# Splitting the first output projection by tokens, with more fill pieces around the small steps and weight splits in quarters

## What is computed

```python
h = _rmsnorm(x, p['norm_mix_pre'])
c = h @ p['w_in']                       # RWKV-7 columns | q k v of attention | two gates
y_a, s_new, shift_new = _rwkv7(c_a, shift_prev, s0, ...)     # per-token matrix state
o = _rmsnorm(softmax(q1 k1) v - lam * softmax(q2 k2) v, p['subln'])
g_a, g_b = jnp.split(jax.nn.sigmoid(g_in + p['b_gate']), 2, axis=-1)
mix = g_a * (y_a @ p['w_out_a']) + g_b * (o @ p['w_out_b'])
x = x + _rmsnorm(mix @ p['w_o'], p['norm_mix_post'])
u_g, u_v = jnp.split(_rmsnorm(x, p['norm_ffn_pre']) @ p['w_ffn_in'], 2, axis=-1)
x = x + _rmsnorm((jax.nn.silu(u_g) * u_v) @ p['w_ffn_out'], p['norm_ffn_post'])
```

## Time and profile before

| | us |
|---|---|
| three timed runs | 1061.17, 1060.76, 1056.54 (median 1060.76) |
| the profiled execution | 1061.27 |
| its span | 1059.4 |
| TensorE (PE) busy | 1008.6 (95%) |
| VectorE (DVE) busy | 488.9 |
| GpSimd (POOL) busy | 486.7 |
| ScalarE (ACT) busy | 275.9 |
| idle time of POOL ahead of w_hi splits, waiting for PE to free a slot | 427.4 |

### The profile page before, as it was taken

The page is one execution under the profiler, slowest core; times in us unless marked ns, Lnnn a source line. Parts: engine busy times, 40 slices in busy tenths (PEclk is TensorE's granted clock), DMA queues, the critical chain, the costliest instruction groups (busy, mean ns, idle before and its releaser), DMA issues.

```text
span 1059.4 us, 21826 instructions
## 1 busy us (share of the span) xinstructions
PE 1008.6 (95%) x8886; PEld 950.9 (90%) x8886; DVE 488.9 (46%) x877; ACT 275.9 (26%) x782; POOL 486.7 (46%) x327
## 2 busy tenths in 40 slices
PE   5999999999889998999999998999999999999997
PEld 4999999977768887878799998999999999999996
DVE  5566799377767455555345254233233332200003
ACT  4223444354433133332211254101001010011111
POOL 3555565432215123142146812655556555566571
PEclk9999999999989999999899999999999999999999
DMA  8222323422213110103313621323232232323332
GB/s 265 61 81 80 84 76 81 132 82 71 65 42 87 33 32 13 53 32 116 110 35 128 189 58 41 99 80 98 79 94 84 81 97 79 92 79 88 92 91 85
DMA packets 137581, 89.16 MB, mean 84 GB/s; under 512 B 5242, under 2 KB 129504, under 8 KB 137504
## 3 DMA queue, kind: packets, MB, share of 16 engines
q1 hardware_dynamic: 128980, 72.65, 24.0%
q10 hardware_dynamic: 8524, 15.42, 4.2%
HBM read 78.86 MB, written 9.19 MB: 83 GB/s over the span
## 4 chain that ended last, share of the span: by engine, by line
PE 81%; DVE 12%; ACT 3%; issue 2%; POOL 1%; DMA 1%; ACTq 0%; DVEq 0%; SPq 0%; POOLq 0%
PE dense L958 65%; PE side L1028 3%; PE side L1148 1%; PE side L910 1%; PE side L874 1%; PE side L884 1%; DVE amax L1635 1%; PE side L1071 1%; PE side L940 1%; DVE otok L1662 1%; DVE early L1650 1%; PE side L864 1%; DVE gt L1756 1%; DVE early L1651 1%; DVE AR L1823 1%
## 5 line engine op out<-in xcount | busy, mean ns | idle before, releaser
L700 POOL TENSOR_SCALAR w_hi<-w_raw 128x1024 fp32r<-128x1024 f32 x117 | 126.8, 1084 | 438.4 <-PE dense L958 427.4
L958 PE MATMUL dense<-h_hi,w_hi 128*128 128x272 f32 (+2 forms) x1392 | 305.9, 297 | 7.3 <-DVE h_lo L1570 5.8
L958 PE MATMUL dense<-h_hi,w_lo 128*128 128x272 f32 (+2 forms) x1392 | 296.5, 291 | 0.0
L958 PE MATMUL dense<-h_lo,w_hi 128*128 128x272 f32 (+2 forms) x1392 | 295.9, 290 | 0.0
L703 POOL TENSOR_TENSOR w_lo<-w_raw,w_hi 128x1024 fp32r<-128x1024 f32 x117 | 286.3, 2447 | 9.8
L958 PEld LDWEIGHTS dense<-h_hi,w_hi 128*128 128x128 f32 x1392 | 223.5, 191 | 18.2 <-issue 6.6
L958 PEld LDWEIGHTS dense<-h_lo,w_hi 128*128 128x128 f32 x1392 | 224.5, 191 | 0.0
L958 PEld LDWEIGHTS dense<-h_hi,w_lo 128*128 128x128 f32 x1392 | 223.1, 192 | 0.0
L958 PE MATMUL dense<-S,w_hi 128*128 128x272 f32 (+2 forms) x648 | 109.2, 289 | 0.0
L958 PEld LDWEIGHTS dense<-S,w_hi 128*128 128x128 f32 x648 | 92.1, 188 | 0.1
L958 PE MATMUL dense<-S,w_lo 128*128 128x272 f32 (+2 forms) x324 | 68.2, 288 | 0.0
(11 more groups left out here) (266 smaller groups left out, 1412.9 us busy)
## 6 DMA issues: line engine op xcount, KB each, us to landing
w_raw<-in_w_ffn_in SPq DMA_DIRECT2D x44, 512.0 KB, 3.7
w_raw<-in_w_in SPq DMA_DIRECT2D x43, 512.0 KB, 3.9
w_raw<-in_w_ffn_out SPq DMA_DIRECT2D x16, 448.0 KB, 3.6
gates<-gst ACTq DMA_DIRECT2D x16, 272.0 KB, 2.0
w_raw<-in_w_o SPq DMA_DIRECT2D x8, 512.0 KB, 4.3
w_raw<-in_w_ffn_out SPq DMA_DIRECT2D x8, 512.0 KB, 3.7
mb<-gates ACTq DMA_DIRECT2D x1, 2176.0 KB, 10.7
ga<-gates ACTq DMA_DIRECT2D x1, 2176.0 KB, 10.2
```

Source lines behind the costliest of these rows:

```text
L700: nc.gpsimd.tensor_scalar(hi, w_raw[:, slot, :], 1.0, 0.0, ALU.mult, ALU.add).then_inc(hi_split, 1)
L958: ins = pe.matmul(acc[:, bk, 0:tn], w, r[:, t0:t0 + tn], start=first and n == 0, stop=final and n == 2)
```

## The change

1. **Fill pieces.** gB and gA quarters are one list, and attention takes 37 of them where it took 32; `turns` gives the 12 places of the last tile 12 pieces where it gave 7. `ofin` takes four fillers where it took five. New fillers stand behind `final` of tile 3, behind `tok` of the sample tile and ahead of its `wu`.
2. **Reciprocals.** For tiles 0 to 2 `yrs` moves from behind `yvar` to the row of `ya`, one level step later; `yfin` comes one place later, behind `ya`.
3. **Output projection by tokens.** Six blocks `outE` (early tokens, output blocks 0 to 5) become fill, between the last steps of the sample tile. Behind the sample's `yfin` stand `outL` 2 to 5 (late tokens alone), `outA` 6 and 7 (all tokens), `outL` 0 and 1. The weights of outL 2 to 5 are still in the two slots; those of 0 and 1 are loaded and split again. The gate `ga` is loaded at outB 0.
4. **mixE.** For outE the mix stays in `mb`; ScalarE and DVE split it into high and low parts in six steps beside woA.
5. **Quarters.** POOL splits each unit after the first and before outE's in 4 + 4 instructions of 128x256 instead of 1 + 1 of 128x1024 (46 units). Semaphores count once a unit as before.

```diff
-DENSE += [(k, i) for k in ("gB", "gA", "outB", "outA", "woA", "woB") for i in range(8)]
+DENSE += [(k, i) for k in ("gB", "gA", "outB") for i in range(8)]
+OUT_EARLY = range(6)
+OUT_LATE = [("outL", 2), ("outL", 3), ("outL", 4), ("outL", 5), ("outA", 6), ("outA", 7), ("outL", 0), ("outL", 1)]
+DENSE += [("outE", i) for i in OUT_EARLY] + OUT_LATE
+DENSE += [(k, i) for k in ("woA", "woB") for i in range(8)]
...
 def state_rows(t):
-    rows = [[s] for s in both("chain0", t)] + [both("q", t), both("ya", t) + both("yb", t)]
+    yrs = [("yrs", t - 1, g) for g in range(2)] if 0 < t < SAMPLE else []
+    rows = [[s] for s in both("chain0", t)] + [both("q", t), yrs + both("ya", t) + both("yb", t)]
...
-    pieces = [dense("gB", i, p, 4) for i in range(8) for p in range(4)]
+    pieces = [dense(k, i, p, 4) for k in ("gB", "gA") for i in range(8) for p in range(4)]
-    turns = [1] + spread(len(pieces) - 1, 3 * len(heads))
+    turns = [1] + spread(24, 3 * BH * SAMPLE) + [2, 1, 1, 1, 1, 0, 1, 1, 1, 1, 1, 1]
...
-    fill = [dense("gA", i, p, 4) for i in range(8) for p in range(4)] + [dense("outB", i, p, 2) for i in range(8) for p in range(2)]
+    fill = pieces + [dense("outB", i, p, 2) for i in range(8) for p in range(2)] + [dense("outE", i) for i in OUT_EARLY]
...
-        s += [("ofin", t)] + filler(1)
+        s += [("ofin", t)] + filler(t < SAMPLE)
...
+                (ymean, yvar, yfin), (f0, f1, f2, f3, f4), (c00, c01, q, ya, c10, c11) = post_rows(t - 1), fills_, state
+                s += weave(invert_rows(t + 1), [c00, ymean, f0, c01, yvar, f1, q, [], f2, ya, f3, yfin, c10, f4, c11])
...
-            s += [("final", t, g) for g in range(2)]
+            s += [("final", t, g) for g in range(2)] + filler(t < SAMPLE)
...
-    s += [dense("outA", i) for i in range(8)]
+    s += [dense(*d) for d in OUT_LATE]
...
-        s += [dense("woA", i)] + ([("zw", "A", i - 1)] if i else [])
+        s += [dense("woA", i)] + ([("zw", "A", i - 1)] if i else []) + ([("mixE", i)] if i in OUT_EARLY else [])
...
+        def pieces(many):
+            return [slice(q * D // many, (q + 1) * D // many) for q in range(many)]
...
+        def split_lo(slot, hi, lo, many=1):
+            for q in pieces(many):
+                ins = nc.gpsimd.tensor_tensor(lo[:, q], w_raw[:, slot, q], hi[:, q].bitcast(F32), ALU.subtract)
+            ins.then_inc(w_split, 1)
...
-            split_lo(u % 2, hi, lo)
+            many = 4 if 0 < u < UNIT_OF[("outE", 0)][0][0] else 1
+            split(u % 2, hi, many)
+            pool.wait_ge(hi_split, u + 1)
+            split_lo(u % 2, hi, lo, many)
...
-                    ops = [(k * P, S[:, k, 0, :], S[:, k, 1, :]) for k in range(KT)]
+                    ops = [(k * P, S[:, k, 0, :], S[:, k, 1, :]) for _, k in OUT_LATE]
...
+                elif kind == "outE":
+                    dve.wait_ge(s_["ga_loaded"], 16)
+                    acc = block_full(dve, d)
+                    a1, mb1 = acc[:, 0, 0:2 * P], mb[:, i, 0:2 * P]
+                    V(vec.scalar_tensor_tensor(out=a1, in0=ga[:, i, 0:2 * P], scalar=1.0, in1=a1, op0=ALU.add, op1=ALU.mult))
+                    block_landed(dve, ("outB", i))
+                    vec.tensor_tensor(mb1, a1, mb1, ALU.add).then_inc(block_sem(d), 1)
```

More of the change, by code:

```diff
@@ L112 @@
 for _kind, _i in DENSE:
-    if _kind in ("outA", "outB"):
+    if (_kind, _i) in OUT_LATE[0:4]:
+        SEGS.append((next(u for u, w in enumerate(UNITS) if w[:2] == ("outE", _i // 2)), _kind, _i))
+    elif _kind in ("outA", "outB", "outE", "outL"):
         if _i % 2 == 0:
@@ L679, in _ @@
                 sp.dma_start(dst.rearrange("p (k n) -> p k n", k=KT), w_in[:, :, c0:c0 + P]).then_inc(raw_loaded[slot], 16)
-            elif kind in ("outA", "outB"):
-                w = w_oa if kind == "outA" else w_ob
+            elif kind in ("outA", "outB", "outE", "outL"):
+                w = w_ob if kind == "outB" else w_oa
                 sp.dma_start(dst.rearrange("p (k n) -> p k n", k=CT), w[:, :, n * 256:(n + 1) * 256]).then_inc(
@@ L981, in dense @@
                 pe.wait_ge(w_split, u + 1)
-                if kind in ("outA", "outB"):
-                    hi, lo = (y_hi, y_lo) if kind == "outA" else (o_hi, o_lo)
+                if kind in ("outA", "outB", "outE", "outL"):
+                    hi, lo = (o_hi, o_lo) if kind == "outB" else (y_hi, y_lo)
                     ops = [(k * 256 + (i % 2) * P, hi[:, k, :], lo[:, k, :]) for k in range(CT)]
                 elif kind in ("woA", "woB"):
-                    ops = [(k * P, S[:, k, 0, :], S[:, k, 1, :]) for k in range(KT)]
+                    ops = [(k * P, S[:, k, 0, :], S[:, k, 1, :]) for _, k in OUT_LATE]
                 elif down:
@@ L996, in dense @@
                 for n in here:
-                    if kind == "outA" and i == 0:
-                        for t in range(NT):
+                    if d in (("outE", 0), OUT_LATE[0]):
+                        for t in EARLY if kind == "outE" else LATE:
                             landed(pe, ("yfin", t, n // 2), "g")
-                    if kind == "woA" and i == 0:
-                        block_landed(pe, ("outA", n))
+                    if d == ("woA", 0):
+                        block_landed(pe, OUT_LATE[n])
+                    if d == ("woB", 0) and n == 0:
+                        pe.wait_ge(s_["mixe_lo"], len(OUT_EARLY))
                     if kind == "down" and i == 0:
@@ L1014, in dense @@
                         places = [(1 - part, *WO_PART["AB"[part]][0:2])]
+                    elif kind in ("outE", "outL"):
+                        places = [(0, *WO_PART["B" if kind == "outE" else "A"][0:2])]
                     elif parts_ == BY_TOKENS:
@@ L1421, in _ @@
                       ACT.Copy).then_inc(s_["y_hi_done"], 1)
+            elif k == "mixE":
+                i = step[1]
+                block_landed(act, ("outE", i))
+                f_act(S[:, i, 0, 0:2 * P], mb[:, i, 0:2 * P], ACT.Copy, scale=0.5).then_inc(s_["mixe_hi"], 1)
             elif k == "zw":
```

88 lines of the change are left out of this document (54 added, 34 removed).

## The result

The changed kernel takes 1053.65 us in the median of 8 runs (1049.86 to 1055.43), the kernel before 1060.49 (8 runs): a ratio of 0.9929, 95% interval 0.9914 to 0.9944, or 7.5 us less. The profiled execution took 1049.86 us (span 1048.1); it is the fastest of the eight, so its trace shows a difference of 11.4 us to the earlier trace rows, of which some 4 are its luck.

A forecast was written before the change was run, and what follows sets the result against it. PE, busy 1008.6 of 1059.4 us, was taken as the bound, leaving idle time and clock falls to gain. The terms -7 - 4.5 - 5 + 4 + 2 = -10.5 took 1061.3 to 1050.8, said as 1051; range 1043 to 1060.

The forecast's parts named there:

- A: Five more gate pieces beside sample attention fill PE's waits and keep the clock: -7 us, between -3 and -8.5.
- C: Three gate pieces put into the sample tile fill short waits and keep the clock: -5 us, between -2 and -6.
- B: Reciprocals moved behind the inversion's subtraction in tiles 1 and 2 end PE's waits: -4.5 us, between -2 and -6.
- D: Output projection by tokens, from the sample tile to woA, adds waits behind the sample: +4 us, between +1 and +7.
- E: POOL's weight splits in quarters cost waits early and free DVE a little in attention: +2 us, between 0 and +8.
- 10.3 us of the work now fills gaps already counted in A to C, so it is charged once, here: In D's sum: the work outE and outB put before yvar, +10.3, was counted once only, giving +4 for D.
- what is late next: In B, tiles 1 and 2: POOL's affine steps start 1.6 us later, but yfin was moved one place back.
- "0" for the extra unit: In D: loading w_out_a five times for four costs POOL 3.45 us and SP one load, on engines 8 us ahead.
- PE waited for little of it that A has not counted: -0.5: In E: DVE saves 2 us a time in attention and at otok scalings, but PE gains only 0.5 us.
- starve: First rival: POOL loses its port turn to DVE up to eight times a split before 200 us; 1072 us, chance 0.10.
- The waits only move: Rival: small-step chains keep their length or quarters leave DVE blocked; A -3, B -2, C -2, total 1060, chance 0.16.
- The late part eats it: Rival: DVE paces outL, the clock falls at the 1.9 us wait, gate loads delay outB; D +9, 1056 us, chance 0.12.

The follow-up runs named there:

- fill-alone trace: The kernel before with only the fill pieces in the changed kernel's places (A and C), nothing else: 1056.14 us, ratio 0.9954 to the kernel before.
- three pairs: Kernels with and without the output projection split: alone 1.0012 to before; in the changed kernel 0.9929 against 0.9915; with quarters from qkv 9 on 0.9910 against 0.9899.

## Why the prediction was right, and where not

The time (1051 forecast, 1053.65 measured) and the sign are right, the ways there mostly not. That the sum came out is in good part luck: against what each part is worth in the changed kernel, A with C and B were forecast 2.9 and 4.5 us too good, D and E 2.5 and 6.7 too bad, and these misses cancel. By part, alone in the kernel before and as lost when undone in the changed one:

| part | forecast | alone | in the changed kernel | of the latter at full clock / clock |
|---|---|---|---|---|
| A + C, fill pieces | -12 | -4.9 | -9.1 | -4.2 / -5.6 |
| B, reciprocals | -4.5 | +4.5 | 0.0 | -1.1 / -0.1 |
| D, output projection | +4 | +1.3 | +1.5 | +6.1 / -5.2 |
| E, quarters | +2 | -4.7 | -4.7 | -2.5 / -2.1 |

The forecast's own signs say the same. PE's idle time between 280 and 560 us was to fall from 21 us to under 10 with the clock at 1.00. It is 21.0, with the clock at 0.98 (0.96 before). The other signs came true, near enough: no wait of over 1 us for xp, no step of DVE in attention over 1.2 us (0.99 at most), 27.1 us from the last yvar product to the first woA matmul for 26.5. By stretches, the three from the inversion of tile 0 to the end of tile 3 idle 16.1 us where they idled 19.3, and the one before woA idles 6.6 for 0.85. So the pieces took work into the same time more than they filled the waits, and the output projection opened new ones.

**A and C: right in place, too large in C.** The fill-alone trace fits A: attention and inversion take in four pieces (6.0 us) and are 2.4 us shorter, 8.4 for a forecast of 7, 5.1 of it clock (forecast 2.5). C's stretch takes two pieces and is 1.1 us shorter: 4.1 of the 5. What failed is the size of the two together, alone and in company.

Pieces are a stock: used earlier, they are missing at the end, where the fill-alone trace has 6.4 us of new idle time and 4.8 more of lost clock. The forecast added A, B and C as if each were worth the same whatever stood beside it, and set only D against them ("10.3 us of the work now fills gaps already counted in A to C, so it is charged once, here"). But outE is not what makes A and C worth 9.1 us in the one place and 4.9 in the other. Without outE, the kernel with A, B, C and E is 9.0 us faster than before, where the parts alone add up to 5.1; and D costs 1.2 to 1.5 us with A and C and without them. The partner is B. Wherever A and C are missing, the parts add up with B at its +4.5: B, D and E together make +1.6 (+1.1 by the parts). Without B, A, C, D and E make -7.6 (-8.3 by the parts). With both, B costs nothing. So A and C are worth 4 to 5 us by themselves, and 9 where they also take away what B costs. Each of these sums is good to 3 or 4 us, so the pattern is as large as its error. A kernel with A, B and C alone would test it and was not run.

**B: the step that failed is "what is late next".** I wrote that POOL's affine steps start later "but yfin was moved one place back", and looked no further than yfin. The waits of 1.25 + 0.39 went, as forecast, and 1.39 and 2.00 us came at the product behind yfin, whose bank y_lo has to clear. "The yfin products come later too, which frees the 0.5 us wait behind them" (-1) had the wrong sign at that same place. And the change reached tile 3 too, where nothing was to be gained: alone, B adds 1.29 and 1.34 us of waits there. In the changed kernel 0.84 of them is left, with the pieces undone 0.68, 0.25 and 1.36. (The terms named for B add up to 5.3, those for C to 5.8; 4.5 and 5 were put into the sum.)

**D: inside its range, wrong parts.** The wait for y_lo was 2.15 for 1.9, the waits between late blocks 1.8 for 2.8. Missed were the split behind the affine steps (1.64, with 0.74 ahead of it) and the shorter lead of w_o (up to 3.3). "0" for the extra unit was wrong for that reason: it costs nothing where it stands and starts all that is behind it 4 us later. Missed on the other side: the clock, 5 us by the account, less with idle PE taken off.

**E: wrong sign.** The costs were sized well. An undisturbed split takes 4.38 us for 3.50 (+0.88, forecast 1.0), and PE loses 3.0 us up to 195 us, forecast 2.5. The step that failed is "PE waited for little of it that A has not counted: -0.5". From the rows I had, I counted the waits that stand in the timeline in front of an instruction of PE. In attention a DVE step sits in nearly each of its chains, and delays of 0.3 to 2 us there come out as small gaps and as stretches of thin work: 4.5 us of attention alone, 3.0 beside the new pieces. Behind attention came the waits for y_lo, in tile 1 above all (3.11 us with whole splits, 1.39 with quarters). The changed kernel's DVE shows what the quarters do: the steps that took 2.37 and 4.21 us in the earlier trace rows take

```profile
276.05 0.37 DVE L1688 SCALAR_TENSOR_TENSOR early<-early,arec 32x160 f32<-32x160 f32 x1
...
296.91 2.32 DVE L1699 SCALAR_TENSOR_TENSOR otok<-otok,orst,subln 128x128 f32<-128x128 f32 x8
```

**The rivals.** POOL did lose turns, but didn't starve. Between 37 and 197 us its splits take 5.48 us on average (3.87 before) and 7.23 at most, for blocks of 6.0; PE waited for one, 0.95 us, besides the one at the start. "The waits only move" was right for B and for nothing else. "The late part eats it" was right in its mechanism, a late part paced by loads, for w_o instead of outB. The clock did fall at the wait for y_lo, as it says (at the lower level from 556.9 to 560.3, behind 2.15 us of idle PE), and over the whole of D the clock still gained.

What stays open: the full-clock and clock parts come from a clock given to three digits (half a us), and count idle PE at the lower level as lost. The sum of the four parts alone (-3.8) is not the -7.5 of all together, and the sums above put the difference on B beside A and C. Why the pieces make B harmless is not shown. The traces show only where its new waits are and that the one in tile 3 is shorter in the changed kernel.

## What to carry to other kernels

Fill work is a stock: a piece moved into an earlier gap leaves a later one, and what replaces it there has its own price. Here that was the split of the output projection, which cost 1.2 to 1.5 us net in three pairs, none of them clear of noise; the kernels without it are as fast. Try a part both alone and by undoing it in company: the reciprocals were +4.5 us by the one and nothing by the other, and a sum of parts would have been wrong either way.

Where an engine that splits or copies in long instructions shares the way to memory with one that sits in the critical chains, cut the long ones up there. It gave 4.7 us by both tests, although the start lost 3.0; leaving the start alone looks like 2 more, which is not clear of the noise. When a step is moved behind a wait, look for who waits for its last product's buffer, not only for its first reader, and at every tile that it moves in. When work is given priority on an in-order queue, check that what it waits for ends first in this very order.

## What was not expected of the hardware

The same change could move several us from one account to the other: outE raised span times clock by 6.2, 6.1 and 6.0 us in three pairs and lowered the rest by 4.6, 5.2 and 5.7 (part of this is idle PE at the lower level; with that taken off, by one trace of each kernel, 6.2, 6.1 and 6.0 become 7.7, 2.5 and 3.2: the same sign, not the same size). In the fill-alone trace PE waits 1.67 us just ahead of the fall and 1.64, 2.54 and 0.96 within the low stretch. That stretch is 17.1 us long (539.6 to 556.6), and about 18 of the 24 matmuls of the first outA block ran in it.

POOL's instructions have a fixed part that the earlier trace rows had not shown apart. A quarter of w_hi takes 0.41 us (a whole 1.05), a quarter of w_lo 0.74 (2.38): both are a fourth of the whole plus 0.15, so six instructions more make the 0.88. The Trainium skill ("GPSIMD Engine Reference", section "Elementwise — side-by-side cycle accounting") gives 2.6 cycles an element for two inputs; by that rate alone cutting would have been free. It names a dispatch for each instruction beside the rate and puts no time to it; the runs show the 0.15.

With quarters DVE and POOL go in turns: where DVE has work, many a quarter of w_hi takes 0.87 us from issue to end, not 0.41. The two sides trade unevenly. Up to 200 us DVE's busy time falls from 135.9 to 113.4 us, for nothing, since PE did not wait for DVE there; behind 196 us the trade is the same in kind and pays. The Trainium skill ("SBUF — State Buffer", section "SBUF: two separate sides") calls the port pair that the two engines share an exclusive lock held for the whole instruction. The traces agree (2.37 us for a DVE step of 0.37 behind a whole w_lo), and the length of the longest instruction (2.4 us whole, 0.74 in quarters) is what the other side risks.
